# One more attention head in flight, a norm in halves, and half a weight panel split at the end of the mixer

## The reference

```python
for i in range(4):                                  # first_block
    h = h + 0.5 * swiglu(rms_norm(h, norm_ffn1[i]), ffn1_w_gate_up[i], ffn1_w_down[i])
    hn = rms_norm(h, norm_mix[i])
    mix = (stick_breaking, moba, mla, stick_breaking)[i](hn, ...)     # 16 heads each
    h = h + mix
    h = h + 0.5 * swiglu(rms_norm(h, norm_ffn2[i]), ffn2_w_gate_up[i], ffn2_w_down[i])
h = rms_norm(h, final_norm)
for i in range(2):                                  # second_block
    proj = rmsnorm(x, norm_mix[i]) @ w_in[i]
    mixed = concat(diff_attention(...), short_conv(...), gla(...))    # 4 heads of 2 maps
    x = x + mixed @ w_out[i]
    x = x + peer(rmsnorm(x, norm_ffn[i]), ...)      # 128 gathered expert rows per token
return rmsnorm(x, norm_final)
```

## Time and profile before

| | |
|---|---|
| median of 3 runs | 4416.1 us (4411.43 to 4416.25) |
| the profiled execution | 4402.66 us |
| its span, first to last instruction | 4400.9 us |
| mean granted TensorE clock | 0.853 of full |
| TensorE busy | 3155.2 us, 72% |
| VectorE busy | 2551.8 us, 58% |
| ScalarE busy | 1104.7 us, 25% |
| GpSimd busy | 1239.2 us, 28% |
| HBM read | 937.45 MB |

### The profile page before, as it was taken

One profiled execution on the slowest core, in us unless ns is written; L12 is line 12 of the kernel. 1 busy time (PEld: TensorE's weight loads), 2 busy tenths in 40 slices (PEclk: granted clock), 3 DMA queues, 4 the chain that ended last, 5 costly groups with the idle time before them and its releaser, 6 DMA issues.

```text
span 4400.9 us, 45074 instructions
## 1 busy us (share of the span) xinstructions
PE 3155.2 (72%) x17054; PEld 2441.9 (55%) x17054; DVE 2551.8 (58%) x4407; ACT 1104.7 (25%) x1509; POOL 1239.2 (28%) x1110
## 2 busy tenths in 40 slices
PE   7999999879998789999998773343345864433433
PEld 6987989848897479898796461111112543111111
DVE  4544554535554445554543468777765458777777
ACT  3333333314332233333432121111101221111110
POOL 0000000000000000000000027778775016778776
PEclk9999999869999889999999687777777877777776
DMA  5623556324643145562354059999999137999999
GB/s 189 207 85 129 185 175 201 109 67 149 205 161 135 46 146 173 177 219 78 131 195 155 0 194 355 349 349 349 349 354 345 39 139 267 362 369 343 352 365 356
DMA packets 415038, 940.88 MB, mean 214 GB/s; under 512 B 27888, under 2 KB 210192, under 8 KB 414864
## 3 DMA queue, kind: packets, MB, share of 16 engines
q0 software_dynamic: 150048, 546.37, 33.7%
q1 hardware_dynamic: 259744, 390.09, 26.2%
q10 hardware_dynamic: 5072, 2.12, 0.2%
HBM read 937.45 MB, written 1.05 MB: 213 GB/s over the span
## 4 chain that ended last, share of the span: by engine, by line
PE 55%; POOL 24%; issue 9%; DVE 6%; DMA 3%; ACT 1%; ACTq 0%; SPq 0%; POOLq 0%; DVEq 0%
POOL wide_ring L2029 24%; PE bank L605 13%; PE bank L606 13%; PE bank L607 13%; PE bank L670 4%; PE bank L649 4%; DMA wide_ring<-in_peer_v,pk_idx 2%; PE bank L655 1%; DVE xn L1402 1%; PE bank L818 1%; PE bank L982 1%; PE bank L811 1%; DVE wide_lo L1292 1%; PE bank L685 1%; DVE x_lo L1416 0%
## 5 line engine op out<-in xcount | busy, mean ns | idle before, releaser
L982 PE MATMUL bank<-wide_ring,xT 128*128 128x512 f32 x960 | 546.1, 704 | 911.8 <-DMA wide_ring<-in_peer_v,pk_idx 911.6
L605 PE MATMUL bank<-x_hi,wide_hi 128*128 128x256 f32 x3328 | 956.0, 287 | 26.4 <-DVE x_lo L1416 26.4
L606 PE MATMUL bank<-x_lo,wide_hi 128*128 128x256 f32 x3328 | 952.6, 286 | 0.0
L607 PE MATMUL bank<-x_hi,wide_lo 128*128 128x256 f32 x3328 | 952.0, 286 | 0.0
L982 PEld LDWEIGHTS bank<-wide_ring,xT 128*128 128x128 f32 x960 | 193.7, 221 | 1262.2 <-issue 1254.2
L2012 POOL TENSOR_TENSOR small<-small,minus_half 128x1 f32<-128x1 f32 (+2 forms) x41 | 27.5, 672 | 2740.3 <-DVE small L1399 2386.3
L1292 DVE TENSOR_TENSOR wide_lo<-wide_ring,wide_hi 128x2048 fp32r<-128x2048 f32 x228 | 521.9, 2289 | 473.1 <-ACT wide_hi L1074 473.1
L2029 POOL DMA_INDIRECT wide_ring<-in_peer_u,pk_idx x512 | 619.8, 1210 | 257.2 <-issue 143.9
L605 PEld LDWEIGHTS bank<-x_hi,wide_hi 128*128 128x128 f32 x3328 | 650.5, 195 | 34.1 <-DVE x_lo L1416 30.5
L606 PEld LDWEIGHTS bank<-x_lo,wide_hi 128*128 128x128 f32 x3328 | 650.7, 196 | 2.7
L607 PEld LDWEIGHTS bank<-x_hi,wide_lo 128*128 128x128 f32 x3328 | 649.9, 195 | 0.0
(11 more groups left out here) (271 smaller groups left out, 3853.4 us busy)
## 6 DMA issues: line engine op xcount, KB each, us to landing
wide_ring<-in_ffn_w_gate_up SPq DMA_DIRECT2D x176, 1024.0 KB, 9.5
deep_ring<-in_ffn_w_down SPq DMA_DIRECT2D x88, 1024.0 KB, 5.0
wide_ring<-in_sb_w_qkv SPq DMA_DIRECT2D x12, 2048.0 KB, 12.3
wide_ring<-in_w_in SPq DMA_DIRECT2D x12, 2048.0 KB, 9.8
wide_ring<-in_peer_w_q SPq DMA_DIRECT2D x8, 2048.0 KB, 17.2
wide_ring<-in_moba_w_qkv SPq DMA_DIRECT2D x6, 2048.0 KB, 12.3
deep_ring<-in_sb_w_o SPq DMA_DIRECT2D x8, 1024.0 KB, 8.2
deep_ring<-in_w_out SPq DMA_DIRECT2D x8, 1024.0 KB, 7.6
```

The source lines that it names most:

```text
L605: mm(o, w[0], x[0], start=start, stop=False, skip_group_check=True)
L606: mm(o, w[0], x[1], start=False, stop=False, skip_group_check=True)
L607: return mm(o, w[1], x[0], start=False, stop=stop, skip_group_check=True)
L982: ins = mm(acc[t][h][:, :], pk_diag[:, s % 2, k], row_at(ph, n)[:, h * 512:(h + 1) * 512], start=first, stop=last, skip_group_check=True)
```

## The change

- Each attention loop has one more head between scores and transposes: TensorE's order becomes scores `i`, transposes (or sums) `i-2`, mix `i-3`, and the other engines follow. For that the probabilities have four buffers (`wide_b`, `m2_b4`) in place of two, and stick-breaking's `z`, `l` and `softplus` three. `out_product` comes one turn later.
- In a norm VectorE makes and announces each tile in two halves (`normed` counts 4), and TensorE waits for halves. Behind a mixer or an ffn the scaling of tile 0's sum is issued in `add_deep`, between the adds of tile 0 and tile 1.
- The first half panel of the phase after the next norm is split at the end of the mixer: ScalarE after the last mix, VectorE ahead of `add_deep`. It goes to slot 1, so in that next phase the two slots change places (`split_at`).
- In `mix2` the load of the expert stage's first panel goes onto SP's queue between the second and the third output-projection load, and the keys are transposed ahead of the output projection.

The core of the diff:

```diff
+        def split_at(ph, j):
+            return 1 - j if ph.n > 1 and phases[ph.n - 2].kind in MIXERS else j
+        def splits_in_mixer(ph):
+            after = phases[ph.n + 2:ph.n + 3]
+            return ph.kind in MIXERS and len(after) > 0
...
                     if ph.kind != "peer":
                         for k in range(4):
+                            if ph.kind == "mix2" and k == 2 and ph.n + 2 < len(phases):
+                                panel(phases[ph.n + 2], 0)
                             load_deep(ph, k, out_weights(ph))
...
             def softmax_heads(ph, qk, v, o):
-                for i in range(HEADS + 3):
+                for i in range(HEADS + 4):
                     if i < HEADS:
                         soft_scores(ph, i, *qk(i))
-                    if 0 <= i - 1 < HEADS:
-                        turn_probs(ph, i - 1, i - 1)
                     if 0 <= i - 2 < HEADS:
-                        mix_values(ph, i - 2, v, core_c)
-                    if i >= 6 and (i - 6) % 4 == 0:
+                        turn_probs(ph, i - 2, i - 2, wide_b)
+                    if 0 <= i - 3 < HEADS:
+                        mix_values(ph, i - 3, v, core_c)
+                    if i >= 7 and (i - 7) % 4 == 0:
...
                 turn_groups(ph, 4, m2_out_groups)
+                pe.wait_ge(S["keys_in"], 32 * (i + 1))
+                turn_groups(ph, 8, pk_groups)
...
-                    early = ph.n > 0 and splits_early(phases[ph.n - 1])
+                    early = splits_early(before) or splits_in_mixer(before)
...
+            def first_half(ph):
+                if splits_in_mixer(ph):
+                    act.wait_ge(S["mixed"], ph.at.get("mixed", 0) + RAISES[ph.kind]["mixed"])
+                    wide_half(phases[ph.n + 2], 0, 0)
...
                 for i in range(HEADS + 2):
                     if i < HEADS:
-                        act.wait_ge(S["probs_T"], seen(ph.at.get("probs_T", 0) + i - 1))
-                        soft_exp(ph, i)
-                    if i >= 1:
-                        move_probs(ph, i - 1)
+                        act.wait_ge(S["probs_T"], seen(ph.at.get("probs_T", 0) + i - 3))
+                        soft_exp(ph, i, wide_b)
+                    if i >= 2:
+                        move_probs(ph, i - 2)
+                first_half(ph)
...
+                    if t == 1 or ph.n == 0 or phases[ph.n - 1].kind not in ADDS:
+                        mean_square(ph, t)
                     dve.wait_ge(S["rstd"], at.get("rstd", 0) + t + 1)
-                    V.scalar_tensor_tensor(out=(resid if to_resid else xn)[:, t], in0=resid[:, t],
-                                           scalar=small[:, 4 + t:5 + t], in1=gains[:, gslot],
-                                           op0=ALU.mult, op1=ALU.mult).then_inc(S["normed"], 1)
+                    for half in range(2):
+                        d0, d1 = half * 512, half * 512 + 512
+                        V.scalar_tensor_tensor(out=(resid if to_resid else xn)[:, t, d0:d1],
...
             def add_deep(ph, n, scale):
                 for t in range(TT):
+                    if t == 1 and ph.n + 1 < len(phases) and phases[ph.n + 1].kind in NORMS:
+                        mean_square(phases[ph.n + 1], 0)
...
+                if splits_in_mixer(ph):
+                    wide_half(phases[ph.n + 2], 0, 0)
                 add_deep(ph, 4, 1.0)
```

More of the change, by code:

```diff
@@ L61 @@
 NORMS = ("norm", "norm_split", "norm_final")
+MIXERS = ("sb", "moba", "mla", "mix2")
+ADDS = (*MIXERS, "ffn")
 BURST = 16
@@ L226, in build @@
         core_c = cut(CORE + 1536, 2, TRI)
-        core_d = cut(CORE - 768, 2, TRI)
-        core_e = cut(CORE - 1536, 2, TRI)
+        sb_z, sb_l, sb_sp = (cut(8192 + 3 * TRI * k, 3, TRI) for k in range(3))
+        sb_arg, sb_w = (cut(11648 + 2 * TRI * k, 2, TRI) for k in range(2))
+        wide_b = cut(12288, 4, TRI)
+        m2_b4 = cut(9472, 4, TRI)
         sb_qT, sb_kT = cut(0, KT, TOK), cut(2048, KT, TOK)
@@ L568, in _ @@
                         sp.wait_ge(S["row_mixed"], ROWS_MIXED * ph.i)
[L569 to L573, removed]
+                    for k in range(len(panels(ph))):
+                        if not (ph.kind == "peer" and k == 0):
+                            panel(ph, k)
                     if ph.kind != "peer":
                         for k in range(4):
+                            if ph.kind == "mix2" and k == 2 and ph.n + 2 < len(phases):
+                                panel(phases[ph.n + 2], 0)
                             load_deep(ph, k, out_weights(ph))
@@ L578, in _ @@
             if last.kind == "norm_final":
[L579 removed]
+                sp.wait_ge(S["normed"], last.at["normed"] + 4)
                 src = xn
@@ L917, in parallel_mixer @@
                 pe.wait_ge(S["moved_odd"], at["moved_odd"] + 2)
-                for u in range(2 * DA_HEADS + 3):
+                for u in range(2 * DA_HEADS + 4):
                     if u < 2 * DA_HEADS:
@@ L1234, in parallel_mixer @@
                 move_turned(act, ph, range(4), move, "moved_even")
-                for u in range(2 * DA_HEADS + 1):
+                for u in range(2 * DA_HEADS + 2):
                     if u < 2 * DA_HEADS:
-                        act.wait_ge(S["probs_T"], seen(ph.at.get("probs_T", 0) + u // 2))
-                        soft_exp(ph, u)
-                    if u >= 2 and u % 2 == 0:
-                        move_probs(ph, u // 2 - 1)
+                        act.wait_ge(S["probs_T"], seen(ph.at.get("probs_T", 0) + u // 2 - 1))
+                        soft_exp(ph, u, m2_b4)
+                    if u >= 3 and u % 2 == 1:
+                        move_probs(ph, (u - 3) // 2)
                 move_turned(act, ph, range(4, 10), move, "moved_even")
+                first_half(ph)
             def product_keys(ph):
@@ L1407, in norm @@
                 elif ph.kind == "norm_split":
-                    early = ph.n > 0 and splits_early(phases[ph.n - 1])
+                    before = phases[max(ph.n - 1, 0)]
+                    early = splits_early(before) or splits_in_mixer(before)
                     if not early and ph.n + 1 < len(phases):
@@ L1548, in softmax_heads @@
             def softmax_heads(ph, scale, o):
-                for i in range(HEADS + 2):
+                for i in range(HEADS + 3):
                     if i < HEADS:
```

142 lines of the change are left out of this document (77 added, 65 removed).

## The result

The changed kernel takes 4295.24 us (median of 4 runs, 4282.45 to 4303.91) where the first takes 4414.35 (4411.43 to 4416.25): ratio 0.9728, 95% interval 0.9701 to 0.9756, 119 us or 2.7% less. The forecast was 4280, the range 4252 to 4335. The profiled execution of the changed kernel took 4303.91 us (span 4302.2), 9 above its median. Lines move by some 20 to 45: L818 is now L837, L1155 is L1182, L1402 is L1432, L1429 is L1469, L1495 is L1535, L1529 is L1571, L1292 is L1321, L2029 is L2074.

The account below looks back on a forecast made before the run. Ffns and expert stages were taken as fixed; gains lay in dependent chains across engines in attention loops and norms. 77 + 11 + 16 + 12 + 19 + 1.5 = 136.5 off 4416.1 gave 4280, range 4252 to 4335.

Parts of the forecast that it names:

- Softmax loops: moba and mla attention loops: one more head in flight gives 2.35 us a head at full clock, 77 us saved together.
- rival (B): A resource left single or double, such as work[2], closes the same cycle; only norms and drains count: 4376; chance 0.06.
- The clock: In the new softmax loops TensorE reaches full clock after three heads; those at half clock add 4.2 us in moba.
- Rival (A): Clock falls in the new loops; a head costs 3.76, softmax saves 24 instead of 77, so 4333; chance 0.2.
- Two of its own signs: In moba and mla: almost no idle before L818, and clock 0.9 or more after the first 10 us.
- Stick-breaking: Two loops: TensorE becomes the limit and a softplus wait goes under the third output product; 5.5 us each, 11 saved.
- mix2: Two loops: a pair falls from 8.05 to 5.3 us, 2.75 x 3 pairs; 8 us each, 16 saved.
- Norms: Four pieces (a) to (d): 12 us behind ffns, 19 behind mixers and mix2; 1.5 for the final norm and another.
- (d): Norm piece: the split, 4.4 us after the last mix, is covered by the last output product's time.
- Rival (C): Shorter norm gaps keep the clock full, so following product phases' starts save 33 us more: 4247; chance 0.1.
- Rival (D): Slower: VectorE's split ahead of add_deep waits for a panel 23 us late in each of six mixers; chance 0.02.
- The expert stages as long as before: Sign for the changed profile: ffns and expert stages, which run on GpSimd and VectorE, keep their length.

Follow-up runs that it names:

- the filling run: First kernel with four unread 64 x 128 matmuls repeated by TensorE in each turn of moba's loop; 4416.35 us, ratio 1.0001.
- The whole-tile run: Changed kernel with VectorE making each norm tile in one instruction again and TensorE waiting for whole tiles; 4311.22 us, ratio 0.9739.
- The front: Both kernels cut behind the first four blocks and their norm, without mix2 and expert stages; first 2353.62 us, changed 2247.53.
- the second part: Two mix2 and two expert stages; both kernels were also cut to these behind one ffn: first 2302.70 us, changed 2287.78.

## Why the prediction was right, and where it was off

- **Softmax loops: 77 forecast, 78.7 measured** (39.6 + 34.1 + 5.0 for the last products). The sum was close partly by luck: moba gave 39.6 where 41.9 was forecast, mla 34.1 where 30.0 was, and the two misses cancel. 2.35 a head was forecast; between output products it is (16.89 - 7.03) / 4 = 2.46 in moba and 2.30 in mla. VectorE's 2.3 is a limit, as forecast, but not the only one. I had written that the copy of head i-3 "falls inside two turns"; it does so only just, and it is what TensorE's transposes wait for. That is rival (B)'s resource, `work[2]`, and it left the gain only because its ring, 2.34 a head in mla, is hardly longer than VectorE's work. I had not worked out that ring, so this agreement is luck as well.
- **The clock: full, but later.** Three heads at half clock were forecast; in moba it was six (to 888), in mla two. Rival (A) did not happen: once up, the clock stays at 1.00 with TensorE busy 45.48 of 51 us. The Trainium skill (page "TensorE: Matmul & The Clock Gate", section "A second HAM failure mode: psum-queue depth-cycling") tells of a kernel with short, frequent idle spells whose clock goes up and down; with 0.5 to 1.2 us idle between groups the new loop's trace shows no such swing. The old loop's does. The prediction put mla's wait "at full clock" and showed one window; the first kernel's windows, in the form of those above, say otherwise, with the same 1.95 us of idle a head in each:

```profile
1516.00:1520.00 4.00, 2.04 (x8) 1.32 (x8) 1.96 (x7) 1.24 (x5) 0.00 (x0) 0.50 0.04 15
...
1548.00:1552.00 4.00, 1.93 (x14) 1.53 (x14) 2.28 (x8) 1.64 (x6) 0.00 (x0) 1.00 0.06 17
```

So part of what mla gained is clock. The forecast was not hurt, since it set out from the measured 97.9, but the evidence against (A) was weaker than it looked.
- **Two of its own signs failed.** Before L837 "almost no idle" was to be seen, and there are 0.5 to 1.2 us; and the clock was to be at 0.9 after 10 us, while moba's reached full in the product that begins 25 us after its first scores.
- **Stick-breaking: 11 forecast, 10.5 measured** (from first scores to last output product 73.2 and 73.0, now 67.8 and 67.9).
- **mix2: 16 forecast, 16.3 measured**, but divided otherwise: 6.3 from the maps of each, 2.0 and 1.7 from the output products, in which the clock reaches full sooner (the first of the four took 9.09 and 9.17 us, now 7.11 and 7.46). The maps gave less than the forecast 8: it took 5.3 us for a pair, under its own 5.6 for TensorE's work. The gain in the product was not forecast and is partly chance: in the filling run, whose mix2 is the first kernel's, the first product took 8.99 and 7.15. The sum is right by luck.
- **Norms: 31 and 1.5 forecast, about 24 measured, the term most mis-sized.** Behind most ffns 1.23 instead of 1.7, behind a mixer 2.46 (mla 2.75) instead of 3.1, behind mix2 2.77 instead of 3.3. "Two instructions of 512 cost 1.29, so nothing" was taken from the adds; the scaling's halves take 1.41 where one instruction took 1.28. And the transposes of the last half ended 1.36 us after it was made (946.04 to 947.40 in the norm behind moba), where I had taken 1.05. The whole-tile run gives the halves' worth as 0.5, not 0.9; the split's place is worth 1.88 behind a mixer. (d), that the split is covered, held.
- **Rival (C)** did not happen: by the mean granted clock of the first 9 us of the 14 product phases, the stretch at half clock adds to 50.6 and 52.4 us in the two profiles of the first kernel and to 56.9 and 47.5 in the two of the changed one, 0 to 6.1 in each phase. No row says what decides it. **Rival (D)** did not: no add waited for a late panel.
- **"The expert stages as long as before"** is the step that can't be closed. The terms as measured sum to 78.7 + 10.5 + 16.3 + 24 = 130; the kernels differ by 119 to 121. The front has all of its share (106.1 against 107.6 from rows: 78.7, 10.5, seven times 1.23, four times 2.46), so the missing 10 lie mostly in the second part, where the gather stretches vary by 26 us between executions and may be some 6 us longer each. Of the 17 us by which the forecast of 136.5 exceeds the 119, about 7 are thus mis-sized terms, the norms above all, and 10 are open.

## What to carry to other kernels

Before a loop is made deeper, write out each ring of resources with the in-order queue of every engine in it: here the copy that frees the only transpose bank stands behind the exponentials of a later head, and that ring limits the new pace as much as the busiest engine does. To learn whether the busiest engine alone holds the pace, take work off it; a busy share near 1 is no proof. If that work goes to another engine, look whether it lands in the ring. And weigh a few per cent by the gaps in the profile, not by the whole time, where one stage of the kernel varies by more than the effect.

## What the runs showed of the hardware

- TensorE at half clock and busy without a pause stayed at 0.50 from 872 to 888 us in moba's loop; the clock rose only in the output product behind it (0.80 in 888 to 892, 1.00 after). In mla it was 0.59 in 1429 to 1433, with TensorE busy 3.85 of 4 us, and 1.00 in 1433 to 1437, after two heads at half clock. No run shows what made the difference.
- At full clock, TensorE idle 0.5 to 1.2 us a head left the clock at 1.00 in mla's new loop; idle 1.95 us a head, it went between 0.50 and 1.00 in mla's old one.
- Four added matmuls on 64 partitions overlapped with scores on the other 64 (both 0.58 us, started 0.02 apart), and a turn at half clock stayed at 5.71 us. The Trainium skill (page "TensorEngine Tiling (Array Packing)", section "Key Properties") says that separate tiles of the array can work in parallel; these rows agree.
- VectorE's scaling of a 128 x 1024 tile: 1.28 us in one instruction, 1.41 in two.
- The stretch of 512 gathers in an expert stage took between 768.8 and 794.6 us in 24 profiled stages. Five runs of the changed kernel spread by 21.0 us, five of its front, which has no such stage, by 9.4.
